# Two changes in the attention stage: weighted values in double runs, and a router that reads unnormalised rows

## The reference, cut to what matters

```python
h   = rms_norm(x, norm_mix_g)
a, gate, q, k, v = split(h @ w_in)
c   = silu(layer_norm(causal_depthwise_conv(a * sigmoid(gate), width=31)))
# 8 heads of 64, stick-breaking weights, strictly causal:
z   = q @ k.T / 8
w   = exp(log_sigmoid(z) + sum of log_sigmoid(-z) over later keys)
o   = rms_norm(w @ v, attn_out_g)
x   = x + concat(c, o) @ w_out
h2  = rms_norm(x, norm_ffn_g)                 # x * rsqrt(mean(x*x) + eps) * g
lg  = h2 @ w_router_group                     # 4 groups
le  = h2 @ w_router_expert                    # 32 experts
# best group, its best two of 8 experts, weights by softmax
x   = x + sum over the two experts of  w_e * (silu(h2 @ w_g) * (h2 @ w_u)) @ w_d
```

## Time and profile before

| | us |
|---|---|
| median of 3 runs | 2188.38 |
| lowest and highest run | 2186.2, 2188.7 |
| span of the profiled execution | 2187.6 |
| PE busy, whole span | 2089.9 |
| DVE busy | 1616.3 |
| ACT busy | 1259.0 |
| POOL busy | 767.6 |

### The profile page before, as it was taken

The page is one execution under the profiler, slowest core; times in us unless marked ns, Lnnn a source line. Parts: engine busy times, 40 slices in busy tenths (PEclk is TensorE's granted clock), DMA queues, the critical chain, the costliest instruction groups (busy, mean ns, idle before and its releaser), DMA issues. The chain is left out here.

```text
span 2187.6 us, 40169 instructions
## 1 busy us (share of the span) xinstructions
PE 2089.9 (96%) x13511; PEld 1763.6 (81%) x13512; DVE 1616.3 (74%) x2084; ACT 1259.0 (58%) x2199; POOL 767.6 (35%) x696
## 2 busy tenths in 40 slices
PE   8999999996899999899999897999999999999998
PEld 6888888885687887678787775888888888888887
DVE  3799999994777667867878868879699556466644
ACT  5322433344677677866676644768678456455533
POOL 1111444553566565645545453211111112111111
PEclk9999999996999999999999998999999999999999
DMA  7563334434333233433222116989899968667851
GB/s 227 190 205 136 120 126 155 133 107 144 108 123 110 80 111 102 115 100 116 80 73 93 54 71 247 377 309 370 299 369 373 305 205 279 216 208 264 286 165 35
DMA packets 211805, 393.17 MB, mean 180 GB/s; under 512 B 54781, under 2 KB 81789, under 8 KB 211677
## 3 DMA queue, kind: packets, MB, share of 16 engines
q1 hardware_dynamic: 198141, 357.42, 47.1%
q0 software_dynamic: 13536, 34.12, 6.6%
HBM read 315.42 MB, written 91.23 MB: 186 GB/s over the span
## 5 line engine op out<-in xcount | busy, mean ns | idle before, releaser
L2528 DVE TENSOR_TENSOR p_w_lo<-p_raw,p_w_hi 128x1024 fp32r<-128x1024 f32 (+1 forms) x196 | 330.3, 1718 | 134.2 <-ACT p_w_hi L2320 133.6
L2124 POOL TENSOR_TENSOR late<-late,p_past 128x1024 f32<-128x1024 f32 (+4 forms) x166 | 308.2, 1857 | 341.9 <-DVE p_past L1981 338.7
L796 DVE SCALAR_TENSOR_TENSOR p_ut<-p_ut,p_cw 128x512 f32<-128x512 f32 (+1 forms) x480 | 329.2, 760 | 0.0
L2320 ACT ACTIVATE p_w_hi<-p_raw 128x2048 fp32r<-128x2048 f32 (+1 forms) x150 | 271.6, 1842 | 62.1 <-PE p_up L2412 53.3
L1981 DVE TENSOR_TENSOR_SCAN p_past<-p_keep,p_past,p_one 128x513 f32<-128x513 f32 (+1 forms) x196 | 225.9, 1192 | 76.6 <-ACT p_keep L1798 74.6
L1798 ACT ACTIVATE p_keep<-p_zp 128x512 f32<-128x512 f32 (+3 forms) x326 | 158.8, 547 | 114.3 <-PE p_zp L1672 101.6
L2412 PE MATMUL p_gp<-p_w_hi,p_xt_hi 128*128 128x256 f32 x736 | 214.3, 291 | 0.0
L473 PE MATMUL p_pj<-p_w_hi,p_xt_hi 128*128 128x512 f32 x512 | 205.2, 401 | 4.2 <-DVE p_xt_lo L772 2.4
L2412 PE MATMUL p_gp<-p_w_lo,p_xt_hi 128*128 128x256 f32 x736 | 206.4, 280 | 0.0
L2412 PE MATMUL p_gp<-p_w_hi,p_xt_lo 128*128 128x256 f32 x736 | 206.4, 280 | 0.0
L473 PE MATMUL p_pj<-p_w_hi,p_xt_lo 128*128 128x512 f32 x512 | 200.6, 392 | 0.0
(11 more groups left out here) (315 smaller groups left out, 5005.2 us busy)
## 6 DMA issues: line engine op xcount, KB each, us to landing
p_raw<-in_w_up SPq DMA_DIRECT2D x96, 512.0 KB
p_raw<-in_w_gate SPq DMA_DIRECT2D x96, 512.0 KB
p_raw<-in_w_down SPq DMA_DIRECT2D x96, 512.0 KB
late<-in_w_up SPq DMA_DIRECT2D x32, 512.0 KB
late<-in_w_gate SPq DMA_DIRECT2D x32, 512.0 KB
late<-in_w_down SPq DMA_DIRECT2D x32, 512.0 KB
wide_raw<-in_w_in SPq DMA_DIRECT2D x56, 256.0 KB, 4.0
wide_raw<-in_x SPq DMA_DIRECT2D x17, 512.0 KB
```

What stands on the lines that cost most here:

```text
L796: dve.scalar_tensor_tensor(dst, src, cw[:, a, j:j + 1], dst, ALU.mult, ALU.add).then_inc(tap_done, 1)
L2124: pool.tensor_tensor(mine, mine, past_rows[:, u % NP, 0:n, 2:2 + w], ALU.mult).then_inc(a_done, 1)
L2320: act.activation(part(w_hi, p, wide), ring(n, wide), ACT.Copy).then_inc(whi_done, wide)
L2528: dve.tensor_tensor(part(w_lo, p, wide), ring(n, wide), part(w_hi, p, wide).bitcast(F32), ALU.subtract).then_inc(wlo_done, wide)
```

## The change

It has two parts.

1. *Values.* `values` of two units of the same query tile run in one go, in every second step, right behind the step's scores and ahead of all its jobs and transposes (`values_at`). The transposed weights are copied back into the slot that the weights came from (`weights_of`), so `at` goes, and the ring of slots grows from 4 to 6. ScalarE's second sigmoids wait for `av_done` of six units before in place of `t_done` of four before; the copies wait no more for `av_done`.
2. *Router.* `h2t` transposes raw y, not h2. The gain is multiplied into the router weights once (`router_gain`), and the inverse root is applied to the logits as they leave PSUM (`route`). The rows for the experts are made beside it: ScalarE multiplies by the inverse root (`scale_rows`), GpSimd by the gain (`hidden`, one operation of 1024 columns). `h2t` is planned 2 steps after `wo` in place of 5, the stores and y reloads come 2 steps later, the planned costs follow, and the tail is written anew.

```diff
-                then = s + 5 if s < end or job[1] == 2 * NT - 1 else s + 2
+                then = s + 2
...
-        NW, NK, NP, NA, NZ = 4, 2, 3, 4, 2
+        NW, NK, NP, NZ = 6, 2, 3, 2
...
+        values_at = {}
+        for i in last:
+            for u in range(first[i], last[i] + 1):
+                values_at.setdefault(min(u + (u - first[i] + 1) % 2, last[i]) + 4, []).append(u)
...
-        square_step = {m: e + 1 if e < end else e for m, e in end_step.items() if m >= NT}
+        square_step = {m: e + 1 if e < end or m == 2 * NT - 1 else e for m, e in end_step.items() if m >= NT}
+        scale_step = {m: s + (3 if s < end else 1) for m, s in square_step.items()}
+        hidden_step = {m: e + (5 if e < end else 2) for m, e in end_step.items() if m >= NT}
+        store_step = {m: e + (7 if e < end else 5) for m, e in end_step.items() if m >= NT}
...
-            y_step[m] = max(y_step[m], end_step[m - 3] + (5 if m - 3 >= NT else 1))
+            y_step[m] = max(y_step[m], end_step[m - 3] + (7 if m - 3 >= NT else 1))
...
-                    pe.wait_ge(h2_done, 2 * r + c + 1)
+                    pe.wait_ge(y_done, 2 * j[1] + c + 1)
                     for k in range(4):
                         last = pe.transpose(bank[:, k * P:(k + 1) * P],
-                                            h2[:, r % 2, (4 * c + k) * P:(4 * c + k + 1) * P], ident[:, :])
+                                            y[:, j[1] % 3, (4 * c + k) * P:(4 * c + k + 1) * P], ident[:, :])
...
                 if s < len(units):
                     scores(s)
+                for u in values_at.get(s, []):
+                    values(u)
                 for j in ahead(s):
                     job(j)
                 if 0 <= s - 3 < len(units):
                     transpose_weights(s - 3)
                 for j in behind(s):
                     job(j)
-                if 0 <= s - 4 < len(units):
-                    values(s - 4)
...
                 if u >= NW:
-                    act.wait_ge(t_done, base[u - NW + 1])
+                    act.wait_ge(av_done, u - NW + 1)
...
                 act.wait_ge(t_done, n + 1)
-                if u >= 2:
-                    act.wait_ge(av_done, u - 1)
-                act.activation(at[:, n % NA, 0:w], tp[:, n % 2, 0:w], ACT.Copy).then_inc(cp_act, 1)
+                act.activation(weights_of(u, x, 0, w), tp[:, n % 2, 0:w], ACT.Copy).then_inc(cp_act, 1)
...
+            def scale_rows(m):
+                r = m - NT
+                act.wait_ge(rs_step, 2 * r + 2)
+                act.activation(h2[:, r % 2, :], y[:, m % 3, :], ACT.Copy, scale=rstd[r % RR]).then_inc(scaled, 1)
...
-                    dve.tensor_copy(lg[:, x, :], bank[:, 0:NG]).then_inc(lg_done, 1)
-                    dve.tensor_copy(le[:, x, :], bank[:, NG:NR]).then_inc(lg_done, 1)
+                    dve.wait_ge(rs_step, 2 * (j[1] - NT) + 2)
+                    scale = rstd[(j[1] - NT) % RR]
+                    dve.tensor_scalar(lg[:, x, :], bank[:, 0:NG], scale, None, ALU.mult).then_inc(lg_done, 1)
+                    dve.tensor_scalar(le[:, x, :], bank[:, NG:NR], scale, None, ALU.mult).then_inc(lg_done, 1)
...
-            def hidden(m, c):
-                r, mine = m - NT, slice(c * C, (c + 1) * C)
-                dve.wait_ge(const_in, 48)
-                dve.wait_ge(rs_step, 2 * r + 2)
-                dve.scalar_tensor_tensor(h2[:, r % 2, mine], y[:, m % 3, mine], rstd, g2[:, mine], ALU.mult,
-                                         ALU.mult).then_inc(h2_done, 1)
...
+            def hidden(m):
+                r = m - NT
+                pool.wait_ge(scaled, r + 1)
+                pool.tensor_tensor(h2[:, r % 2, :], h2[:, r % 2, :], g2[:, :], ALU.mult).then_inc(h2_done, 1)
```

More of the change, by code:

```diff
@@ L1248, in phase_attend @@
         q_lo = sb("q_lo", [P, 2, HG, P], F32R)
-        wgt = late.all.rearrange("p (n l) -> p n l", n=NW)
-        at = sb("at", [P, NA, 4 * P])
+        wgt_rest = sb("wgt_rest", [P, NW - LATE // UW, UW])
+        slots_of = [late.all[:, n * UW:(n + 1) * UW] for n in range(LATE // UW)]
+        slots_of += [wgt_rest[:, n, :] for n in range(NW - LATE // UW)]
         kd = sb("kd", [P, 3, HG, HD])
@@ L1277, in phase_attend @@
         go = sb("go", [P, CT])
-        st = sb("st", [P, 16])
+        st = sb("st", [P, 15 + RR])
         oms, orr, ort = st[:, 0:4], st[:, 4:8], st[:, 8:12]
-        ss, rt, rstd = st[:, 12:13], st[:, 13:14], st[:, 14:15]
+        ss, rt, rstd = st[:, 12:13], st[:, 13:14], [st[:, 14 + n:15 + n] for n in range(RR)]
         mhalf = sb("mhalf", [P, 4])
@@ L1380, in phase_attend @@
             dve = 7 * w + sum(dve_cost.get(j[0], 0) for j in jobs[s]) + 4 * (s - 1 in o_step_of)
-            act += 10 * sum(1 for m, e in end_step.items() if m >= NT and e == s - 1)
-            dve += 10 * sum(1 for half in hidden_step for e in half.values() if e == s)
+            act += 10 * sum(1 for m, e in square_step.items() if e == s) + 10 * sum(1 for e in scale_step.values() if e == s)
             dve += 30 * sum(1 for e in pick_step.values() if e in (s - 1, s - 2))
@@ L1858, in _ @@
                     squares(m)
+                for m in at_step(scale_step, s):
+                    scale_rows(m)
         @block.vector
@@ L2028, in _ @@
             for s in range(steps):
-                for c in (1, 0) if s < len(units) else (0, 1):
-                    for m in at_step(hidden_step[c], s):
-                        hidden(m, c)
                 for n in at_step(piece_step, s - 1):
@@ L2147, in _ @@
                     rank_constants()
+                if s == first[NT] // 2 + 4:
+                    router_gain()
                 for m in at_step(split_step, s):
@@ L2154, in _ @@
                         inverse_rms(m)
+                for m in at_step(hidden_step, s):
+                    if s < end + 5 or m == 2 * NT - 1:
+                        hidden(m)
                 if s < len(units):
@@ L2159, in _ @@
                 early_homes(*home_step.get(s, (0, 0)))
+                if s == end + 7:
+                    hidden(2 * NT - 2)
             pool.wait_ge(home_done, 2 * EARLY)
```

70 lines of the change are left out of this document (39 added, 31 removed).

## The result

The kernel after takes 2198.3 us against 2188.3 of the kernel before, a ratio of 1.0043 (1.0031 to 1.0055): 0.4% slower where 0.8% faster was forecast. Medians are over 4 runs each; the profiled execution spans 2195.6 us, 8.0 more than before.

A forecast was written before the change was run, and what follows sets the result against it. TensorE, 96% busy, was taken to set the pace, in the attention stage too. Terms of -28.7 - 4 + 12 - 3 + 11.5 - 4 + 2 - 3 gave -17.2 us: span 2170.4, median 2171, range 2154 to 2187.

The forecast's parts named there:

- Term 1: Attention stage: 82 of 166 runs of values go, each saving 0.35 us of crossing: 28.7 us less.
- Term 2: Behind a run of values: mostly transposes follow instead of scores and pay less for the crossing: 4 us less.
- Term 3: Steps left without values: scores wait for ScalarE's sigmoids, 12 us more, bounds 8 and 16.
- Term 4: Three places behind steps that get double values: scores' existing waits for sigmoids go, 3 us less.
- Term 5: Runs of values: the second unit's product waits for late copies of its weights, 11.5 us more, bounds 4 and 20.
- Term 7: The tail after the last y: logits and attention output come earlier, 3 us less, bounds 0 to 5.
- Term 6: Router: VectorE's lost `hidden` operations give 4 us less, ScalarE's scalings 2 more; GpSimd's multiplications and the y reload nothing.
- the subtraction: Timeline of 80 steps losing their values, with values and crossings taken out: 35 waits of scores, 15.2 us in all.
- ScalarE's price: Router: ScalarE's 17 added scalings push the next sigmoids in steps without a wo job, 2 us more, bounds 0 to 6.
- (a): Rival: waits for sigmoids and copies at upper bounds add up and eat the saving, +3 us, 2192; chance 0.15.
- (b): Rival: those waits hardly appear, through ScalarE's lead and VectorE's relief, -40 us, 2148; chance 0.15.
- (c): Rival: GpSimd's multiplications make VectorE's picks later, 20 us in all, sum +6.8, 2195; chance 0.08.

The follow-up runs named there:

- values' half alone: Only the change's values edits (grouped runs, six buffers, copies in place) on the kernel before: 2192.2 us, ratio 1.0013.
- router's half mended: Only the router's edits on the kernel before, with y reloaded earlier and the tail's order changed: 2193.5 us, ratio 1.0019 against the kernel before.
- the 25 pairs: Values' half, grouping only pairs whose valueless step has its wo matmuls behind the transposes: 2187.7 us, ratio 1.0005 against the kernel before.
- fewer values: Kernel before, leaving out one key tile's values in every second unit, nothing grouped: 2180.8 us, ratio 0.9971.

## Why the prediction was wrong, by its steps

The forecast was -17.2 us of span, and 8.0 more were measured, 25.2 us apart. By the account above, crossings give 8.0 us less than terms 1 and 2 had, scores' waits 14.1 more than terms 3 and 4, late copies 5.4 more than term 5, the tail 9.4 more than term 7, and the other waits 7.3 less than term 6: 29.6 us, where the account is good to some 5.

**Term 1 held in its size per run, roughly.** A crossing costs 0.31 us (49.3 over 159 runs), not 0.35: 24.7 us in place of 28.7.

**Term 2 was no gain.** A crossing is no cheaper after (24.6 us over 81 runs, 0.30 each). Where the scores no longer pay 0.11 us behind a run, a part of it is now a wait of their later matmuls for a sigmoid: these waits inside the scores go from 4.4 to 12.9 us.

**Term 3, scores for sigmoids, failed in size.** At the first matmul of a step the subtraction was good: 5.7 us of waits before, 20.3 after, 17.9 of them behind steps without values, where it had given 15.2. I then cut it to 12, and left out the waits inside the scores: 23 us in all (19 with the median distances), beyond the upper bound of 16. Term 4's three waits did not show as a gain: scores are later in total.

**Term 5, late copies, failed in size.** 16.9 us against 11.5, inside its bounds. The raw count, 19.9, was nearer; I had taken 8.4 off as waits that were there anyway.

**Term 6, the router, failed in sign and place.** The reload of y was costed at nothing with a bound of 3, with its condition named right (wo seven steps behind the wo of three tiles before) and not looked up in the plan, where one tile meets it exactly. It cost 6.5 us of TensorE alone and 2.1 together. The relief of VectorE, put at 4 us, is there at single places (7 us near 1255 us in the router's half mended), but no gain is left at the last scores: they start 2.2 us later than before with the router's half mended, and 1.6 us later in the kernel after than with the values' half alone. ScalarE's price can't be told from these.

**Term 7, the tail, failed in sign.** 6.4 us more instead of 3 less. The last y, squares and logits went as worked out; what stood queued ahead of the last normalise on GpSimd, and that the picks of the fourth batch came earlier in the new table, was not followed. Nor was it that GpSimd's last multiplication meets the last picks.

Of the rivals, (a) came nearest in its mechanism: the waits ate the saving. It gave 2192 for both halves together, which took 2198.3; that the values' half alone took 2192.2 is a coincidence of numbers, since (a) also charged ScalarE's scaling. It was given 0.15 and argued down with "each wait lets ScalarE and VectorE catch up", which the sums don't show. The -40 us of rival (b) hold only if ScalarE's 2 us are left out; with them the sum is -38. Rival (c), a chance of 0.08 and 2195, has its mechanism too: small pick operations beside GpSimd are lengthened by 12.3 us in all after, where before had 5.4, 7 us in place of 20. In the tail 2 us of it reach TensorE, as the rows above show; for the rest nothing shows that they did.

What stays open: what the mended router's half loses ahead of 1248 us, why the 25 pairs gain so little, when the clock falls behind a wait and when not, and the worth of a third bank with short scans.

## What to carry to other kernels

A run taken out of a step is also a cover taken away: group operations only in steps where other work fills the gap, and here the same edit made with that condition went from no gain to 0.25% and 0.37%. When a load's earliest step is moved, list its lead for every tile from the plan; the one tile with none was the only one that waited for its load. Follow the last wait through every queue: in the tail, links taken one at a time changed nothing in the time, and taken together they shortened it by 4.4 us. Before an edit is priced by one profiled execution, compare the granted clock of both in windows.

## What the runs showed of the hardware

Going over to tiles of 64 columns and back costs 0.31 us a run. The Trainium skill ("TensorEngine Tiling (Array Packing)", Key Properties) says that changing the tiling mode drains TensorE, without a price; the trace agrees in that every change costs time.

A scan whose constant lies in PSUM is not held by GpSimd (1265 ns alone, 1273 beside it); with all operands in SBUF it took 1264 ns alone and 2111 beside it, 1746 in the mean, and the kernel 54 us more. The Trainium skill ("SBUF — State Buffer", SBUF: two separate sides) gives the rule: GpSimd and an operation of VectorE with two SBUF inputs, or in a two-port performance mode, hold an exclusive lock against each other for a whole instruction. The scans agree. So do the small pick operations: one of 8 columns with two SBUF inputs took 1.31 and 1.54 us beside GpSimd's multiplication in place of 0.17. A cast of 24 columns, which has one input, was held too, for 2.42 us; no row tells the mode that it ran in.

Equal waits of TensorE of some 1.5 us left the clock full in one kernel and at 0.57 for 12 us in the next. Such falls move by 5 us what an edit elsewhere seems to bring. They also part executions of one kernel: the six with fewer values took 2176.7 us at a mean clock of 0.984 and 2185.0 at 0.978.
